# Low and high weight parts handed out one slab per mixed tile at the end of the first block's mixers

## What is computed

```python
y = jax.nn.sigmoid(g_merge_a) * (from_heads(o_fox) @ w_fox_o) + jax.nn.sigmoid(g_merge_b) * (o_gla @ w_gla_o)
return y @ w_out
...
h = h + rmsnorm(mix, g_post_mix[l])
h = h + 0.5 * rmsnorm(swiglu(rmsnorm(h, g_pre_ffn2[l]), w_ffn2_gu[l], w_ffn2_down[l]), g_post_ffn2[l])
```

## Time and profile before

| | |
|---|---|
| median of 3 executions | 2423.27 us (2422.98 to 2424.35) |
| the profiled execution, its own time | 2424.13 us |
| its span | 2422.8 us |
| mean granted clock of PE | 0.996 of full speed |
| PE busy | 2381.7 us, 98% |
| DVE busy | 1646.3 us, 68% |
| ACT busy | 1239.8 us, 51% |

### The profile page before, as it was taken

How to read it: one execution, slowest core, us unless ns; L and a number is a source line. 1 busy time by engine, 2 the same in 40 slices (tenths; PEclk the granted TensorE clock), 3 DMA queues, 4 the chain that set the end, 5 groups by cost and what they waited for, 6 DMA issues and landing times.

```text
span 2422.8 us, 45847 instructions
## 1 busy us (share of the span) xinstructions
PE 2381.7 (98%) x18834; PEld 2288.6 (94%) x18834; DVE 1646.3 (68%) x2919; ACT 1239.8 (51%) x2084; POOL 52.3 (2%) x102
## 2 busy tenths in 40 slices
PE   8999999999999999999999999999999999989999
PEld 7999988999999998899999999889999999978999
DVE  6656877775486568777756875776765767584764
ACT  5444555554464445555544654565544655455542
POOL 2001100000000011000000000000000010000000
PEclk9999999999999999999999999999999999999999
DMA  7654633465556554356655664434665676532763
GB/s 208 177 177 130 162 88 109 127 193 178 174 155 176 178 146 128 89 156 165 185 190 152 194 186 151 125 104 124 192 188 169 169 203 200 163 105 74 208 188 132
DMA packets 588720, 382.79 MB, mean 158 GB/s; under 512 B 44719, under 2 KB 564371, under 8 KB 588512
## 3 DMA queue, kind: packets, MB, share of 16 engines
q1 hardware_dynamic: 585360, 376.77, 53.7%
q0 software_dynamic: 3152, 3.08, 0.5%
HBM read 378.66 MB, written 1.07 MB: 157 GB/s over the span
## 4 chain that ended last, share of the span: by engine, by line
PE 89%; DVE 6%; ACT 2%; issue 1%; DMA 1%; SPq 0%; DVEq 0%; ACTq 0%
PE bank L584 88%; DVE wlo L2004 1%; ACT whi L1327 1%; DVE ry L2023 0%; DVE ry L2021 0%; PE bank L914 0%; DVE ybuf L2054 0%; DVE smh L2438 0%; PE bank L682 0%; DMA wraw<-in_w_ffn_gu 0%; DVE hT L2058 0%; DVE xlo L2037 0%; DMA wraw<-in_ffn_w_gate 0%; DVE ssum L2016 0%; DVE rst L2025 0%
## 5 line engine op out<-in xcount | busy, mean ns | idle before, releaser
L2004 DVE TENSOR_TENSOR wlo<-wraw,whi 128x1024 fp32r<-128x1024 f32 (+2 forms) x723 | 866.2, 1205 | 285.9 <-ACT whi L1327 283.2
L1327 ACT ACTIVATE whi<-wraw 128x1024 fp32r<-128x1024 f32 (+2 forms) x723 | 747.8, 1043 | 591.4 <-DMA wraw<-in_w_ffn_gu 170.6
L584 PE MATMUL bank<-xhi,whi 128*128 128x256 f32 (+3 forms) x3928 | 583.2, 288 | 11.3 <-ACT whi L1327 4.0
L584 PE MATMUL bank<-xhi,wlo 128*128 128x256 f32 (+3 forms) x3928 | 570.5, 285 | 7.2 <-DVE wlo L2004 7.2
L584 PE MATMUL bank<-xlo,whi 128*128 128x256 f32 (+3 forms) x3928 | 560.8, 284 | 0.0
L584 PEld LDWEIGHTS bank<-xhi,whi 128*128 128x128 f32 (+2 forms) x3928 | 514.7, 188 | 30.2 <-issue 9.0
L584 PEld LDWEIGHTS bank<-xhi,wlo 128*128 128x128 f32 (+2 forms) x3928 | 514.5, 188 | 10.6 <-DVE wlo L2004 10.2
L584 PEld LDWEIGHTS bank<-xlo,whi 128*128 128x128 f32 (+2 forms) x3928 | 510.1, 187 | 0.2
L584 PE MATMUL bank<-act_hi,wlo 128*128 128x256 f32 (+1 forms) x1408 | 400.6, 284 | 0.0
L584 PE MATMUL bank<-act_lo,whi 128*128 128x256 f32 (+1 forms) x1408 | 400.4, 284 | 0.0
L584 PE MATMUL bank<-act_hi,whi 128*128 128x256 f32 (+1 forms) x1408 | 398.6, 283 | 0.0
(11 more groups left out here) (408 smaller groups left out, 1830.5 us busy)
## 6 DMA issues: line engine op xcount, KB each, us to landing
wraw<-in_w_ffn_gu SPq DMA_DIRECT2D x176, 512.0 KB, 3.9
wraw<-in_w_ffn_down SPq DMA_DIRECT2D x88, 512.0 KB, 3.2
wraw<-in_ffn_w_gate SPq DMA_DIRECT2D x88, 512.0 KB, 4.0
wraw<-in_ffn_w_up SPq DMA_DIRECT2D x88, 512.0 KB, 3.9
wraw<-in_ffn_w_down SPq DMA_DIRECT2D x88, 512.0 KB, 3.3
wraw<-in_w_in SPq DMA_DIRECT2D x80, 512.0 KB, 3.8
wraw<-in_a_w_in SPq DMA_DIRECT2D x24, 384.0 KB, 3.3
wraw<-in_w_out SPq DMA_DIRECT2D x16, 512.0 KB, 3.8
```

Of the source, the lines that this page charges most:

```text
L584: return E.matmul(out_, lhsT, rhs, start=first, stop=last, skip_group_check=True)
L1327: A.activation(flat(whi, u), flat(wraw, u), ACT.Copy).then_inc(S("hi"), 1)
L2004: V.tensor_tensor(flat(wlo, u), flat(wraw, u), flat(whi, u).bitcast(F32), ALU.subtract).then_inc(lo_ready[u % RING], 1)
```

## The change

In the loop over s, both engines lose the two calls of `ahead` at its top, and get one call per tile d instead. With slabs counted from b, AT of the first slab of s is b + 2s, so the calls say:

| | before, at the top of s | after, ahead of each tile |
|---|---|---|
| ACT, done up to (not with) | b+2s+6 (two slabs) | b+2s+6 for q = 0, b+2s+7 for q = 1 |
| DVE, done up to | b+2s+5 (two slabs); b+12 for s = 3 (three) | b+2s+5 for q = 0, b+2s+6 for q = 1 |

On both engines q = 0 reaches what the top of s reached before, except on DVE at s = 3, and q = 1 one slab more; what is asked for at q = 1 was asked for at the next s before, again but for s = 3.

```diff
@@ scalar_program, mixer1
             for s in range(4):
-                for name in MIX_OUT[L]:
-                    ahead((name, L, s))
                 for q in range(2):
                     d = 2 * s + q
+                    hi_until(AT[MIX_OUT[L][0], L, s] + 6 + q)
                     if d + 2 < KD:
                         sigmoids(d + 2)
                     A.wait_ge(S("mix"), KD * L + d + 1)
@@ vector_program, mixer1
             for s in range(4):
-                for name in MIX_OUT[L]:
-                    ahead((name, L, s))
-                if s == 3:
-                    lo_until(AT["wo", L, 0] + HEAD)
                 for q in range(2):
                     d = 2 * s + q
+                    lo_until(AT[MIX_OUT[L][0], L, s] + 5 + q)
                     for z, name in enumerate(MIX_OUT[L]):
                         g = 0 if name == "fo" else 1
```

## The result

| | before | after |
|---|---|---|
| median of 11 executions each | 2423.27 us (2418.75 to 2425.28) | 2430.16 us (2428.70 to 2432.34) |
| profiled execution, its own time | 2424.13 us | 2429.76 us |
| its span | 2422.8 us | 2428.4 us |
| granted clock of PE, mean | 0.996 | 0.995 |

The change makes the kernel slower: the ratio is 1.0027, 95% interval 1.0019 to 1.0035, so 4.6 to 8.5 us. I had forecast 2429.1 us.

The account below looks back on a forecast made before the run. PE, 98% busy, bounds the kernel, losing time in `head` where it waits for DVE's low part of b+11. Waiting 4.43 plus half clock 1.36 gave +5.8 us on 2423.3: 2429.1 us, range 2425.8 to 2431.8.

Parts of the forecast that it names:

- DVE's order at s = 3: In `head`, PE's eighth matmul waits one tile longer for b+11's low part: +2.25 us layer 0, +2.18 layer 1.
- One count: In `head`, PE was said to want tile 6 only at k = 6, 76 less 8 matmuls after the eighth.
- The other low parts: On DVE at s = 0 to 2, b+5, b+7 and b+9 move one tile earlier, pushing tiles 1, 3, 5 back 1.14 us; no cost.
- the new wait in layer 1: At `head`'s start PE waits 0.9 us for tile 5's products; price nothing while the later wait stands.
- ACT: ACT makes each second slab's high part a tile earlier; it has room, `xhi` is not later behind its sum; no cost.
- One sign that I named: In layer 1's `head`, PE's wait of 1.32 us for b+10's high part at 1088.13 was to vanish; worth nothing.
- The clock: Around `head`'s longer pause, half clock lasts twice as long, 5.0 us with PE at work: +1.4 us for both layers.
- The sum: On the profiled execution, 4.43 us of waiting and 1.36 of half clock make +5.8 us: 2424.1 becomes 2429.9.
- (1): In `head`, the clock recovers while PE stands: 2426.0 us in both layers, 12%; 2427.5 in one, 15%.
- (2): More half clock, in a layer or at the second block's pauses: +1.5 us each, 2430.6 to 2432.1 us; 10%.
- (3): In `head`, PE waits on high parts or loads, not on the low parts' order: 2423.3 us; 3%.
- The fourth: Low parts slip into DVE's 0.57 us wait for `xhi`, costing half of themselves: 4 us less per layer; 3%.

Follow-up runs that it names:

- the one slab put back: The kernel after with b+11's low part put back ahead of tile 6 in each layer, all else the same: 2423.20 us, ratio 0.9996 against before.
- the doubled dose: The kernel after with b+10's low part moved behind tile 6 and b+11's behind tile 7: 2433.83 us, ratio 1.0044 against before.
- DVE's half: The kernel after with ACT's calls put back as before, so only DVE's calls changed: 2431.73 us, ratio 1.0034 against before.
- ACT's half: The kernel before with only ACT's calls changed: 2423.45 us against 2423.40, ratio 1.0001.
- the filled wait: The kernel after with unused matmuls filling PE's waits in `head`: 2426.52 us, ratio 1.0012 against before; a first form with float32 operands took 2446.69 us.
- the last two runs: The kernel after with low parts made between a tile's sum and its `xlo`: 2416.22 us; then also further ahead, b+11's at tile 5: 2414.97 us.

## Why the prediction was right

*DVE's order at s = 3.* One tile more ahead of b+11's low part was to cost 2.25 and 2.18 us; the table gives 2.17 in layer 0 and 2.25 in layer 1. It is shown by the one slab put back, which undid it all, and by the doubled dose, which added one more tile to the way. One count was off without effect: PE wants tile 6 after 64 matmuls of `head` (two times 8, then four times 12), not after 76, and that is still long after the eighth.

*What I costed at nothing.* The other low parts and the new wait in layer 1: nothing, shown by the run with one slab put back. ACT: nothing alone, shown; `xhi` was never later behind its sum (0.57 us stays at each tile). One sign that I named did not come: I had the wait of 1.3 us for a high part in layer 1 gone, and 1.31 stands there, now for b+11. I had asked only what b+10's high part does. It costs nothing for the reason that I gave, that the low part ends last. What I also didn't see is that DVE's new order, without ACT's, would wait three times 0.43 us for a high part. In the change both come together, so the sum was not touched.

*The clock.* I took twice the stretch, and it was twice the stretch, in both layers. That was in part luck. The three profiles with a low part behind tile 6 (after, DVE's half, the doubled dose) have stretches of 6.8 us five times and of 10.2 once. The three without (before, ACT's half, one slab put back) have 3.4 us four times, but also none and 6.8 once each. So longer waits went with more half clock, but the length of the wait alone did not set the stretch, and why it differed between profiles with the same short waits is open. The size was off: 0.68 us more per layer was forecast, about 0.9 found. I had let the clock fall at 442.8, where it fell before, which is 443.7 with the 0.90 us by which this profile runs late; it fell at 444.2, later into the pause, and so more of its 6.8 us met PE at work, 5.5 instead of 5.0 (a loss of 2.5 instead of 2.2 at the 0.45 of the rows). The rule of the Trainium skill (TensorE: Matmul & The Clock Gate, Terms), half of the time at the lower clock, gives an estimate of 2.8 us for the 5.5, and of 3.4 for the whole stretch of 6.8. The matmuls' own pace, 0.227 against 0.125 us, gives 2.5, and the filled wait, 2.5 us shorter in layer 0, agrees with that. That the clock causes this share, and isn't only seen beside it, the filled wait shows.

*The sum.* 5.8 forecast on the profiled execution, 5.6 measured, of which 6.3 in the two stages; that the sum came so close is partly chance, since 0.90 us ahead of the stage and 1.6 us regained in the second block have nothing to do with it. Against the medians 5.8 forecast, 6.9 measured, inside the interval.

*The rivals.* The clock did not come back at once (1), no stretch was longer than 6.8 us (2), and PE did wait for low parts (3). The fourth couldn't come true with the call where the change puts it, as its refutation said, and the last two runs show that its mechanism is real once the call is moved: the forecast there was half a low part per tile, and 0.67 us of 1.14 was found.

## What to carry to other kernels

When work of an engine that runs behind is spread more evenly, ask for each piece who waits for it: here six of the seven low parts cost nothing in their new places, and the seventh was moved behind a tile that nobody needed yet. Count the instructions ahead of the piece that is wanted first, before and after. And before reordering around a wait between two engines, look whether work that has no part in that wait can be put inside it: the same low parts one instruction earlier turned a loss of 0.27% into a gain of 0.30%.

## What the runs showed of the hardware

In the changed stage half clock came in stretches of 3.4 or 6.8 us in these profiles; with the doubled dose one of 10.2 us stood in layer 1, from 1092.9 to 1103.1, though PE's pause had ended at 1099.5. With the doubled dose the way to the eighth matmul is some 2 us longer than in after, and half clock costs less, since only 4.2 and 3.6 us of it met PE at work, against 5.5 and 5.6. Between executions of one kernel the whole time spread by 6.5 us (before, 11 executions), more than the changed stage costs, and the profiles show at least one source: the second block's stretch near 1531 lasted 6.8 us in the profile before and 3.4 us in the one after, with the same code.
